# Where the plain one-hot operand of the gate matrices is written: VectorE or GpSimd

## The reference, cut to what matters

```python
act = gelu(einsum('nd,nkd->nk', xc, u_tab[ec]))       # up row of each chosen expert
return einsum('nk,nkd->nd', gc * act, v_tab[ec])      # weighted sum of the down rows
```

## Time and profile before

| | |
|---|---|
| median of 3 runs | 4115.94 us (4110.73 to 4116.23) |
| profiled execution, its own time | 4109.24 us |
| its span in the trace | 4106.3 us |
| mean granted TensorE clock | 0.951 of full speed |
| bytes read from HBM | 1226.75 MB |
| TensorE, VectorE, GpSimd busy | 91%, 61%, 18% of the span |

### The profile page before, as it was taken

The page is one execution under the profiler, slowest core; times in us unless marked ns, Lnnn a source line. Parts: engine busy times, 40 slices in busy tenths (PEclk is TensorE's granted clock), DMA queues, the critical chain, the costliest instruction groups (busy, mean ns, idle before and its releaser), DMA issues.

```text
span 4106.3 us, 50824 instructions
## 1 busy us (share of the span) xinstructions
PE 3720.2 (91%) x21387; PEld 3138.3 (76%) x21387; DVE 2509.0 (61%) x4071; ACT 289.5 (7%) x733; POOL 758.2 (18%) x629
## 2 busy tenths in 40 slices
PE   6899799999997899897995779999998998999997
PEld 4677677777786688785884668888887887888886
DVE  3319920002589986765888857666667666666765
ACT  1010110010000010000001200000000000000000
POOL 1000000000000022331232214222323222232320
PEclk9899899999999899997997989999999999999999
DMA  9564344475432269996786879999999999999995
GB/s 333 210 251 172 130 177 183 169 268 189 154 134 88 88 268 399 410 418 258 297 325 248 309 280 421 421 421 421 419 421 414 421 421 401 421 420 421 419 408 229
DMA packets 205019, 1258.35 MB, mean 306 GB/s; under 512 B 20040, under 2 KB 53312, under 8 KB 53991
## 3 DMA queue, kind: packets, MB, share of 16 engines
q1 hardware_dynamic: 84631, 611.24, 38.3%
q0 software_dynamic: 85648, 616.08, 36.7%
q10 hardware_dynamic: 34512, 27.79, 2.1%
HBM read 1226.75 MB, written 28.64 MB: 306 GB/s over the span
## 4 chain that ended last, share of the span: by engine, by line
DMA 39%; PE 35%; DVE 20%; issue 4%; POOL 1%; ACT 0%; DVEq 0%; SPq 0%; ACTq 0%; POOLq 0%
PE banks L581 24%; DMA arena<-peer_v,arena 22%; DMA arena<-peer_u,arena 14%; PE banks L860 6%; DVE arena L1235 3%; DVE arena L1225 3%; PE banks L604 2%; POOL arena L509 1%; PE banks L563 1%; DMA arena<-w_ada 1%; DVE arena L1889 1%; PE banks L886 1%; DVE arena L1523 1%; DVE arena L1886 1%; DVE arena L1533 0%
## 5 line engine op out<-in xcount | busy, mean ns | idle before, releaser
L860 PE MATMUL banks<-arena 128*128 128x256 f32 x8192 | 1799.5, 382 | 86.5 <-DVE arena L1913 60.9
L860 PEld LDWEIGHTS banks<-arena 128*128 128x128 f32 x8192 | 1568.2, 192 | 310.8 <-issue 75.4
L581 PE MATMUL banks<-arena 128*128 128x288 f32 (+1 forms) x6464 | 1536.5, 399 | 36.1 <-DVEq L1206 28.8
L581 PEld LDWEIGHTS banks<-arena 128*128 128x128 f32 x6464 | 1237.0, 193 | 305.1 <-DVEq L1206 30.3
L1235 DVE SCALAR_TENSOR_TENSOR arena<-arena 128x2048 f32<-128x2048 f32 x285 | 670.2, 2351 | 383.8 <-DMA arena<-peer_v,arena 381.6
L1225 DVE SCALAR_TENSOR_TENSOR arena<-arena 128x2048 f32<-128x2048 f32 x288 | 655.2, 2292 | 259.5 <-DMA arena<-peer_u,arena 242.7
L509 POOL DMA_INDIRECT arena<-peer_u,arena x288 | 404.2, 1404 | 1946.7 <-DVE arena L1225 921.9
L509 POOL DMA_INDIRECT arena<-peer_v,arena x288 | 327.6, 1138 | 810.7 <-DVE arena L1235 728.9
L563 PE MATMUL banks<-arena 128*128 128x128 f32 (+4 forms) x445 | 84.5, 331 | 77.1 <-DVEq L1877 27.3
L1116 ACT ACTIVATE arena<-banks 128x256 f32<-128x256 f32 x128 | 48.7, 383 | 1400.8 <-PE banks L860 1400.8
L563 PEld LDWEIGHTS banks<-arena 128*128 128x128 f32 (+4 forms) x445 | 56.9, 165 | 104.2 <-DVEq L1877 27.7
(11 more groups left out here) (254 smaller groups left out, 1619.8 us busy)
## 6 DMA issues: line engine op xcount, KB each, us to landing
arena<-peer_ut SPq DMA_DIRECT2D x128, 1024.0 KB, 9.3
arena<-peer_vd SPq DMA_DIRECT2D x128, 1024.0 KB, 9.2
arena<-w_ada SPq DMA_DIRECT2D x96, 1024.0 KB, 7.2
arena<-w_in SPq DMA_DIRECT2D x96, 1024.0 KB, 4.8
arena<-w_out SPq DMA_DIRECT2D x32, 1024.0 KB, 8.9
arena<-peer_wq SPq DMA_DIRECT2D x32, 1024.0 KB, 4.8
arena<-w_proj_b SPq DMA_DIRECT2D x16, 1024.0 KB, 5.1
arena<-w_proj_a SPq DMA_DIRECT2D x16, 1024.0 KB, 8.0
```

The lines of the kernel that those rows point to most:

```text
L581: last = mm(out, w, src[:, b, :], start=k == 0, stop=k == len(blocks) - 1)
L860: last = mm(dense_out(m), slab16[j][:, k, :], rows[:, k, :], start=k == 0, stop=k == KD - 1)
```

## The change

GpSimd writes the plain one-hot operand, one instruction per token, and VectorE only the weighted one. VectorE signals once, when `slot_rows` stands (`slot_rows_in`); GpSimd signals each token (`plain_ready`), and TensorE waits for both operands. GpSimd's gathers of `peer_u` become a generator, so that they can be issued up to a given count: up to 148 ahead of the first group, then two after every block, and the rest behind the last group.

```diff
-            for hd in range(HEADS):
-                pool.wait_ge(s["head_ready"], hd + 1)
-                for k in range(TOPK):
-                    gather("peer_u", 0, TOPK * hd + k)
-            for k in range(128):
-                gather("peer_u", 1, k)
-            for k in range(32):
-                gather("peer_u", 2, k)
+            def up_rows():
+
+                for hd in range(HEADS):
+                    pool.wait_ge(s["head_ready"], hd + 1)
+                    for k in range(TOPK):
+                        gather("peer_u", 0, TOPK * hd + k)
+                        yield
+                for k in range(128):
+                    gather("peer_u", 1, k)
+                    yield
+                for k in range(32):
+                    gather("peer_u", 2, k)
+                    yield
+
+            rows = up_rows()
+
+            def gathers(upto):
+
+                while ring.n < upto:
+                    next(rows)
+
+            gathers(AFTER_LATE + 4)
+            pool.wait_ge(s["slot_rows_in"], 1)
+            for q in range(TP // 4):
+                if q >= 2:
+                    pool.wait_ge(s["g_made"], q - 1)
+                for j in range(4):
+                    n = 4 * q + j
+                    nc.gpsimd.tensor_scalar(hot[q % 2][0][:, j, :], lane, slot_rows[:, 1, n:n + 1], None,
+                                            ALU.is_equal).then_inc(s["plain_ready"], 1)
+                if q % 4 == 3:
+                    gathers(AFTER_LATE + 4 + 2 * (q // 4))
+            gathers(U_END[2])
             for k in range(128):
                 gather("peer_v", 0, k)
...
                 pe.wait_ge(s["onehot_ready"], q + 1)
+                pe.wait_ge(s["plain_ready"], 4 * q + 4)
...
             settle()
             pf.settle()
+            dve.sem_inc(s["slot_rows_in"], 1)
             for q in range(TP // 4):
                 if q >= 2:
                     dve.wait_ge(s["g_made"], q - 1)
-                did(tt(hot[q % 2][0], bc(lane, 1, 4), bc(slot_rows[:, 1, 4 * q:4 * q + 4], 2, 128), ALU.is_equal))
                 for j in range(4):
```

More of the change, by code:

```diff
@@ L111 @@
 glu_ready pooled yb_ready ya_ready piece_done merged_ready out_ready rows_laid state_rows state_out prompt_out x1_ready
-head_ready keys_laid expand_ready xn_ready dve_stood gt2_ready x1_saved gt2_saved late_ready late_exp slots_laid
+head_ready keys_laid expand_ready xn_ready dve_stood gt2_ready x1_saved gt2_saved late_ready late_exp slots_laid slot_rows_in plain_ready
 onehot_ready g_made g_read h_read gate_done sum_read dense_done buf_used act_ready gelu_ready acc_ready fin_in
```

## The result

| | before | after |
|---|---|---|
| median, 4 runs each | 4113.33 us | 4181.56 us |
| ratio | | 1.0168, 95% interval 1.0152 to 1.0183 |
| profiled execution's span | 4106.3 us | 4176.3 us |
| the gate stage | 209.6 us | 273.8 us |

The forecast was 4136 us, with a range of 4088 to 4215. The time lies inside the range, but the loss is 68 us where 20 were forecast. The page of the kernel after, part 1: GpSimd has 256 instructions more (629 to 885) and 185 us more of busy time, VectorE 64 instructions fewer.

The account below looks back on a forecast made before the run. In the gate stage VectorE was busiest, with GpSimd becoming the later writer: 4 x 1.67 + 6.0 + 0.3 + 1.35 = 14.3 us a block against 13.1, 16 times, +20: 4129 profiled, 4136 us median, range 4088 to 4215.

Parts of the forecast that it names:

- GpSimd becomes the later writer, and TensorE waits for it: Gate stage: a group takes 1.67 us on GpSimd against VectorE's 1.26, so GpSimd finishes later in every group.
- A comparison costs 0.38 us: GpSimd's 128x128 comparison, start to start: VectorE's 0.278 plus 0.10 of a one-element fill.
- The bounds: Limits for one GpSimd comparison: 0.10 us from a one-element fill, 1.24 us from a gather with its issue.
- The 0.15 us between groups: Gap until the next group, added to GpSimd's four comparisons: 4 x 0.38 + 0.15 = 1.67 us.
- The stretch at the end of a block, 6.0 + 0.3 us: GpSimd's fourth comparison shut out by a dot product, then two gathers: 6.0 us; second dot product held back 0.3.
- The waits for the dense product, 1.35 us a block: Writers' waits while TensorE is in a dense product, kept as before: 21.6 / 16 = 1.35 us a block.
- The gathers' place costs nothing by itself: Rows used one block later: gathers land 7.4 to 11.9 us after issue, which a block of 14 us covers.
- The part behind the stage moves one to one: The 1600 us behind the gate stage keep their length, so the stage's change moves the end by as much.
- The faster rival: GpSimd keeps up, comparison 0.30 us or less, nothing trapped: -17 us, 4091 to 4106, say 4099; chance 0.28.
- The shut-out rival: Both engines' comparisons exclude each other in the stage: block 18.8 us, +91 us, 4207; chance 0.20, including much dearer comparisons.
- my likeliest case: GpSimd late and trapped under dot products in the stage: +3 to +38 us, 4119 to 4154; chance 0.42.
- The sign that the prediction had set for this rival: VectorE's weighted one-hots (L1889) stretched beyond 0.28 us from start to start would show the shut-out rival at work.

Follow-up runs that it names:

- one-input steps: Changed kernel with the stage's 32 VectorE dot products replaced by sums of the row alone: 4135.38 us, 1.0061 of before, stage 229 us.
- the half split: Against the kernel before, GpSimd writes the plain operand of two tokens of four, VectorE the other two in one operation: 4103.27 us, 0.9985 of before.

## Why the prediction was wrong in size and right in kind

- **GpSimd becomes the later writer, and TensorE waits for it:** right. GpSimd waits for TensorE 23 us of 274.
- **A comparison costs 0.38 us:** this is the step that failed. It is 0.585 from start to start. Put in the prediction's own sum, 4 x (4 x 0.585 + 0.15) + 6.3 + 1.35 = 17.6 us a block, 16 x (17.6 - 13.1) = 72 us of loss, where 68 were measured. I had taken the nearest row by shape, VectorE's comparison, and added the fixed part of a one-element fill (0.10). (The 0.278 is 1.11 / 4; within a group of four the starts are 0.256 us apart.) But shape didn't carry the duration from one engine to the other: GpSimd's slope is 2.4 ns a column, where VectorE's fast kind has about 0.5 ((1282 - 342) / 1920, from the earlier trace rows), and its fixed part is 0.29. The bounds were 0.10 and 1.24; the middle of those would have been nearer.
- **The 0.15 us between groups** is not there on GpSimd, which runs 16 comparisons in 9.39 us when nothing holds it: 10 us too much in the sum, over 64 groups.
- **The stretch at the end of a block, 6.0 + 0.3 us:** right in size, 4.0 + 2.45 measured, and wrong in order. I had the held comparison slip in between the two dot products, and the gathers held in their turn. In 11 blocks it is held for both (4.6 us), in five one comparison is held for the first and another for the second, and the gathers then run freely: 0.94 to 1.07 us each, not 1.9 and 2.7 as beside dot products in the earlier trace rows.
- **The waits for the dense product, 1.35 us a block:** 23.2 / 16 = 1.45, near by luck: they are GpSimd's, six of 3.9 us, where the 1.35 came from 17 of VectorE's.
- **The gathers' place costs nothing by itself:** shown by the run with only that moved. In the stage of the changed kernel no dot product waits for its row.
- **The part behind the stage moves one to one:** nearly. The stage lost 64 us and the span 70, within the 10 us of difference that the prediction had allowed. In the stage and the 41 us behind it 1 MB less was fetched ahead (72.0 against 71.0, by the stretches' GB/s and lengths), 2.4 us at 415 GB/s; the other 3 us are open.
- **The faster rival** (0.30 us or less) is refuted by the 0.590 of the shortest comparison. The estimate after the GPSIMD Engine Reference of the Trainium skill, 0.19 us for 128 elements before dispatch, is not what this instruction does: 2.4 ns a column at the page's 1.2 GHz would be 2.9 cycles, an estimate, and not 1.8.
- **The shut-out rival** forecast 0.66 us a comparison in effect or a loss of 91 us, and it is nearer in size than my likeliest case; but its cause is not the one at work. VectorE's comparisons have grown by 7 us in all (0.370 on average, 0.343 in the earlier trace rows) and GpSimd's by 0.016 us each. The sign that the prediction had set for this rival, VectorE's comparisons beyond 0.28 us from start to start, did come, barely: a group of four takes 1.18 us (median) and not 1.11, 0.29 each. It is not where the loss is, for VectorE waits 114 us in the stage. The exclusion does exist one way: in the run with one-input steps, four of VectorE's that started amid a row of GpSimd's took 2.45 us and not 1.11, with 0.58 us from one to the next, GpSimd's own pace.

```profile
2250.84 4.66 POOL L552 TENSOR_SCALAR arena<-arena 128x128 f32<-128x128 f32 x8
...
2251.99 2.45 DVE L1918 TENSOR_SCALAR arena<-arena 128x128 f32<-128x128 f32 x4
```

## What to carry to other kernels

An idle engine is a helper up to the point at which its own line (here 16 comparisons, a hold, two gathers) is as long as that of the engine it relieves; work out both lines per block, for each share, and take the share at which they meet. Then check in the trace which of them waits: at the half split the sum had GpSimd as the slower one, and it was VectorE. Three tokens of four on GpSimd were not run. Half of the work gave 6 us and all of it cost 68. A duration that no row shows should be bounded from rows of the same engine, and where the sign hangs on it the width of those bounds is the forecast. Before giving work to another engine, look whether the waits come from too few buffers: one more set was worth 14 us by itself.

## What the runs showed of the hardware

- A GpSimd comparison of 128 partitions with a scalar per partition, float32: 0.44 us for 64 columns, 0.597 for 128, 0.528 for 128 with the number in the instruction (medians).
- Such a comparison that begins 0.31 us into a VectorE operation with two inputs from SBUF is held through that one and through the next, which follows at once (4.6 us, 11 blocks). One that begins 0.01 us before the first is held through that one alone (2.70 us), and the next comparison through the second (2.40 us, five blocks). Under a sum over the row, of the same length with one input, the longest is 0.708. That agrees with the rule of the Trainium skill (SBUF — State Buffer, "Who interferes with whom").
- The same section says that a VectorE operation in a two-port mode and GpSimd shut each other out. VectorE's comparison is of a fast kind, and here most groups of four ran in 1.16 to 1.31 us in the changed kernel, against 1.11 alone, the longest in 1.69; with one-input steps three of 64 took 2.4 to 2.6. GpSimd's own comparisons took 0.608 us beside VectorE's work and 0.592 without.
